# Low parts of fetched y all on GpSimd, low parts of weights meanwhile all on VectorE

## What is computed

```python
y = jnp.concatenate([ya, yb, ym], axis=-1) * jax.nn.silu(gate)   # first layer
x = x + y @ w_out_even[e]
...
y = jnp.concatenate([yc, ym], axis=-1) * jax.nn.silu(gate)       # second layer
x = x + y @ w_out_odd[o]
```

## Time and profile before

| | |
|---|---|
| median of 3 runs | 2347.54 us (2346.05 to 2352.45) |
| profiled execution | 2350.05 us, span of its instructions 2348.3 us |
| TensorE matmul busy | 2267.7 us (97%) |
| TensorE weight load busy | 1929.2 us (82%) |
| VectorE busy | 1595.3 us (68%) |
| ScalarE busy | 1311.1 us (56%) |
| GpSimd busy | 683.4 us (29%) |
| mean granted TensorE clock | 0.995 |

### The profile page before, as it was taken

How to read it: one execution, slowest core, us unless ns; L and a number is a source line. 1 busy time by engine, 2 the same in 40 slices (tenths; PEclk the granted TensorE clock), 3 DMA queues, 4 the chain that set the end, 5 groups by cost and what they waited for, 6 DMA issues and landing times.

```text
span 2348.3 us, 35371 instructions
## 1 busy us (share of the span) xinstructions
PE 2267.7 (97%) x11778; PEld 1929.2 (82%) x11778; DVE 1595.3 (68%) x3262; ACT 1311.1 (56%) x3038; POOL 683.4 (29%) x843
## 2 busy tenths in 40 slices
PE   7999999999999999999999999899999999999999
PEld 6888788888888878888888888787787888887887
DVE  7443677777886433346665566658888888889787
ACT  6444566666775434456656566654656645455542
POOL 3455232311245542222222221565563200000000
PEclk9999999999999999999999999999999999999999
DMA  7322111111243342223232322533343632345734
GB/s 228 116 74 65 40 28 33 32 34 48 61 129 107 95 138 62 93 68 91 89 95 72 93 88 87 192 90 113 102 145 108 190 102 92 115 146 168 232 114 138
DMA packets 332355, 241.68 MB, mean 103 GB/s; under 512 B 66448, under 2 KB 284816, under 8 KB 331664
## 3 DMA queue, kind: packets, MB, share of 16 engines
q1 hardware_dynamic: 332176, 239.43, 33.6%
HBM read 195.59 MB, written 43.78 MB: 102 GB/s over the span
## 4 chain that ended last, share of the span: by engine, by line
PE 78%; DVE 11%; ACT 4%; issue 3%; DMA 2%; SPq 1%; POOL 1%; DVEq 0%; ACTq 0%; POOLq 0%
PE PS L1938 14%; PE PS L1940 14%; PE PS L1939 14%; PE PS L2168 6%; PE PS L2170 6%; PE PS L2169 6%; PE PS L2084 5%; PE PS L2051 5%; PE PS L2038 3%; PE PS L2039 2%; ACT PY L2179 1%; PE PS L2093 1%; PE PS L1993 1%; PE PS L2075 1%; DVE ST L2547 1%
## 5 line engine op out<-in xcount | busy, mean ns | idle before, releaser
L2844 POOL TENSOR_TENSOR WS<-WR,WS 128x256 fp32r<-128x256 f32 x635 | 491.9, 794 | 995.8 <-ACT WS L2179 993.1
L1938 PE MATMUL PS<-HT,WS 128*128 128x512 f32 x1492 | 601.6, 403 | 15.6 <-POOL WS L2844 5.5
L1940 PE MATMUL PS<-HT,WS 128*128 128x512 f32 x1492 | 583.9, 391 | 0.0
L1939 PE MATMUL PS<-HT,WS 128*128 128x512 f32 x1492 | 581.7, 390 | 0.0
L1938 PEld LDWEIGHTS PS<-HT,WS 128*128 128x128 f32 x1492 | 280.9, 188 | 73.1 <-issue 10.4
L1940 PEld LDWEIGHTS PS<-HT,WS 128*128 128x128 f32 x1492 | 280.3, 188 | 61.4
L1939 PEld LDWEIGHTS PS<-HT,WS 128*128 128x128 f32 x1492 | 281.4, 189 | 52.0
L2179 ACT ACTIVATE PT<-PS 128x512 fp32r<-128x512 f32 x352 | 186.2, 529 | 199.2 <-PE PS L2051 198.7
L2179 ACT ACTIVATE WS<-WR 128x256 fp32r<-128x256 f32 x658 | 245.6, 410 | 91.0 <-PE PS L1940 55.2
L2437 DVE TENSOR_TENSOR PT<-PS,PT 128x512 fp32r<-128x512 f32 x352 | 211.2, 609 | 84.7 <-ACT PT L2179 81.8
L2084 PE MATMUL PS<-PT,QKV 128*128 128x256 f32 (+1 forms) x1248 | 208.8, 289 | 3.2 <-DVE YB L2616 2.3
(11 more groups left out here) (284 smaller groups left out, 4573.2 us busy)
## 6 DMA issues: line engine op xcount, KB each, us to landing
WR<-in_w_in_odd SPq DMA_DIRECT2D x106, 256.0 KB, 2.9
EO<-in_grid SPq DMA_DIRECT2D x48, 384.0 KB, 3.0
WR<-in_ffn_in SPq DMA_DIRECT2D x60, 256.0 KB, 3.0
WR<-in_w_in_even SPq DMA_DIRECT2D x100, 128.0 KB, 2.5
WR<-in_w_out_odd SPq DMA_DIRECT2D x48, 256.0 KB, 2.9
yd<-PY SPq DMA_DIRECT2D x44, 256.0 KB, 3.4
EO<-in_ffn_in SPq DMA_DIRECT2D x35, 256.0 KB, 3.0
WR<-in_w_in_even SPq DMA_DIRECT2D x34, 256.0 KB, 2.9
```

The costliest lines, as they stand in the source:

```text
L1938: e.matmul(out, wh, rh, start=start, stop=False)
L1939: e.matmul(out, wh, rl, start=False, stop=False)
L1940: return e.matmul(out, wl, rh, start=False, stop=stop)
L2844: e.tensor_tensor(ws(i, 1, n), RAW[raw_slot(u)][:, o:o + n], f32(ws(i, 0, n)), ALU.subtract).then_inc(s_wlop.sem, 1)
```

## The change

A new entry of the planner's state, `at["back"]`, is set from the start of the last chunk to the end of the products that run beside it. While it is set, every new weight split gives its low part to VectorE (`s_wlov`); before, GpSimd had them all here (the other condition, `at["second"]`, is not yet set in these two layers). And all low parts of fetched y are GpSimd's (`s_ylp`), where every second one was VectorE's. The list of steps, the high parts, the transfers, the buffers and the matmuls are the same.

```diff
             def last_chunk(att, upto, end, loads):
                 left, owed = 16, 0.0
+                at["back"] = True
                 next(loads)
...
             run_upto(end)
+            at["back"] = False
             ht_after[0] = (s_mm, s_mm.n)
...
                 if no < at["both"]:
                     on = s_wlov if no % (2 if no < 2 * MEM_UNITS else 3) else s_wlop
                 else:
-                    on = s_wlov if at["second"] and no >= at["second"] and no % 4 == 3 else s_wlop
+                    on = s_wlov if at["back"] or at["second"] and no >= at["second"] and no % 4 == 3 else s_wlop
                 half_lo.append((on, on.add()))
                 put("split", no)
...
                     s_yh.add()
-                    on = s_ylv if back % 2 else s_ylp
+                    on = s_ylp
                     i, d = landed[back]
```

More of the change, by code:

```diff
@@ L367, in build @@
         units, subs, half_lo, used = [], [], [], {}
-        at = {"load": 0, "split": 0, "both": 0, "bank": 0, "ys": 0, "slot": 0, "task": 0, "gen": None, "piece": 0, "rope": False, "f1": False, "one": False, "deep": None, "second": None}
+        at = {"load": 0, "split": 0, "both": 0, "bank": 0, "ys": 0, "slot": 0, "task": 0, "gen": None, "piece": 0, "rope": False, "f1": False, "one": False, "deep": None, "second": None, "back": False}
         raw_at = []
```

## The result

The changed kernel takes 2356.82 us (2354.06 to 2358.93) beside 2348.63 us for the kernel before (2346.05 to 2352.45). The ratio is 1.0036, with a 95% interval of 1.0025 to 1.0047, so it is slower by 8.5 us (5.9 to 11.0). That lies above my range. The profiled execution took 2358.05 us, with a span of 2356.1 us against 2348.3.

The account below looks back on a forecast made before the run. TensorE, 78% of the chain that ended last, was taken as the bound. First layer -0.5 and second layer +1.1 summed to +0.6 us, with clock 0: 2348.1 us as a median, range 2341.5 to 2353.5.

Parts of the forecast that it names:

- The bound: Two stages, one per layer: TensorE idle 5.1 and 10.2 us, clock falls 3.4 us, 18.7 us at stake in all.
- my signs: What the new profile should show, such as idle of both stages together at 15 to 17 us.
- the wait at L2093: Second layer, TensorE before transposes: 2.8 us now, weight load issued 2.1 us later, so +1.5 us; over 5 would favour (B).
- (B): Rival: y parts in a row on GpSimd delay fetches and weight loads through SyncE, 8.4 us slower, 2355.9 us; chance 0.12.
- Who changes hands: Per layer, 36 weight parts to VectorE and 11 y parts to GpSimd: VectorE busy +7.7 us, GpSimd -12.5 us.
- The holding: VectorE ops with two SBUF inputs and GpSimd ops lock a shared port; a weight part beside y costs up to 1.37 us.
- First layer: Sum of the first layer's stage: y4 to y7 about 0, the wait before 700.79 +0.2, other waits gone; -0.5 us.
- the wait at 700.79: First layer, TensorE's 1.81 us wait for a GpSimd weight part; forecast to change by +0.2 us.
- the two smaller waits there: First layer, TensorE's other two waits for GpSimd weight parts behind a y part, 0.7 us, forecast to go.
- Second layer: Sum of the second layer's stage: +0.2 + 1.5 - 0.6 = +1.1 us, bounds -3 and +4.
- Clock: TensorE's clock falls to half in both stages: change taken as 0, bounds -3.4 (both gone) and +1.7 us (one more).
- (A): Rival: TensorE's 5.5 us weight waits and 1.2 us y4 wait go, clock stays up; up to 10.1 us faster, 2337.4; chance 0.20.

Follow-up runs that it names:

- four fills: The changed kernel with each GpSimd low part of y replaced by four fills of 256 columns, which read no SBUF: 2345.47 us, ratio 0.9990 to the kernel before.

## Why the prediction was wrong

**The bound** held. The loss is idle time and clock of the same two stages; outside them the matched instructions drift by under 1.5 us. Of my signs, idle of both stages together came out at 20.2 us in the two windows of 80 us, where I had said 15 to 17, and the wait at L2093 stayed under the 5 us that would have spoken for (B).

**Who changes hands** held in count. VectorE's busy time seems to agree too: +7.7 us forecast for each layer, +7.0 in the 80 us of the first, +7.7 in the second. That is luck, since the changed kernel does less of its work within the same 80 us. Over the whole span VectorE's busy time grew by 20.8 us (1595.3 to 1616.1), 10.4 for each layer, as my sum had priced every part as if nothing held it. GpSimd's fell by 30.2 us (683.4 to 653.2), 15.1 for each layer against my 12.5: in the kernel before its own instructions were being held as well.

**The holding** I had read, with its 1.37 us and with the exclusive lock of the Trainium skill (SBUF — State Buffer, section "SBUF: two separate sides"). The same page of the Trainium skill (section "Who interferes with whom") says that a VectorE instruction with two SBUF inputs contends with a GpSimd instruction that reads SBUF and not with one that only writes it. The fills bear that out (0.43 us at most beside them). The 1.37 us I had called about the rest of the GpSimd instruction plus 0.42; by the earlier trace rows the rest was 1.16, so the sum is 1.58. But I used the holding as a price of one weight part here and there, and the adds of the sink, with two SBUF inputs too, had no price at all. I never counted what it would hold in total, and this is the step that failed: the sum of the first layer came to -0.5 us, with VectorE's late weight parts at +0.2 us, where TensorE waited 8.3 us for them. The groups of VectorE by line, 680 to 765 us (count | busy us, mean ns): first the kernel before, then the changed one, then the one with four fills.

```profile
L2675 DVE TENSOR_TENSOR HT<-PY,HT 128x512 fp32r<-128x512 f32 x5 | 6.5, 1295 | 2.8 <-ACT HT L2179 2.8
L2675 DVE TENSOR_TENSOR HT<-EO,HT 128x512 fp32r<-128x512 f32 x3 | 4.8, 1607 | 0.0
...
L2576 DVE TENSOR_TENSOR ST<-ST 128x1 f32<-128x1 f32 x18 | 2.8, 155 | 0.0
L2675 DVE TENSOR_TENSOR QKV<-EO,QKV 128x512 fp32r<-128x512 f32 x2 | 2.7, 1368 | 1.1 <-ACT QKV L2179 1.1
...
L2675 DVE TENSOR_TENSOR QKV<-PY,QKV 128x512 fp32r<-128x512 f32 x1 | 0.9, 857 | 0.3 <-ACT QKV L2179 0.3
```

```profile
L2470 DVE TENSOR_TENSOR WS<-WR,WS 128x256 fp32r<-128x256 f32 x36 | 23.7, 701 | 6.9 <-ACT WS L2181 6.9
...
L2578 DVE TENSOR_TENSOR ST<-ST 128x1 f32<-128x1 f32 x18 | 5.9, 330 | 0.0
```

```profile
L2470 DVE TENSOR_TENSOR WS<-WR,WS 128x256 fp32r<-128x256 f32 x36 | 13.6, 418 | 13.3 <-ACT WS L2181 13.3
...
L2578 DVE TENSOR_TENSOR ST<-ST 128x1 f32<-128x1 f32 x18 | 2.8, 154 | 0.0
```

In the kernel before, VectorE was held for 14.9 - 11 x 0.68 = 7.4 us in y parts, which TensorE needs later than the next weight part, and next to nothing elsewhere; the adds had none (155 ns). In the changed kernel it is held for 23.7 - 13.6 = 10.1 us in weight parts and 5.9 - 2.8 = 3.1 in adds. The total nearly doubles, and it moves to parts that TensorE needs next.

**First layer, -0.5 us forecast, 6.6 measured with this layer changed alone (5.9 in the matched traces).** I followed the early batches of y with care (y4 to y7, and the wait at 700.79) and found little there. Rightly: the wait that was 1.81 us is 1.4 us now. (For y6 and y7 I wrote 0.6 us later where my own subtraction gave 0.5; it changes nothing.) I gave the later pairs no line of their own. The two new waits, 4.95 us at 713.49 and 1.9 us near 736, both stand behind a finish of attention whose adds meet a row of y parts. Held time is about half of the first, and 1.6 us of the second (adds of 0.80 and 1.11 us in place of 0.16). I had said of the two smaller waits there "they go"; they went, and larger ones came in their place.

**Second layer, +1.1 us forecast, about 2 by difference** (8.5 - 6.6, with some 3 us of uncertainty). The matched traces show 3.4 us, of which the longer fall of the clock is 1.7. The chain that I named was right. The wait at L2093 grew from 2.8 to 3.6 us, against my +1.5, and by way of a late weight load. Two weight parts on VectorE, held to 2.20 us together, ended at 1501.43; but SyncE had a y fetch ahead of the load, issued at 1501.22 once GpSimd's y part had freed its buffer, and this ended last, as I had said. SyncE issued the load at 1501.64 and ScalarE idled 2.45 us for it (the last line is SyncE's waits, 1498 to 1502 us):

```profile
1499.23 2.20 DVE L2470 TENSOR_TENSOR WS<-WR,WS 128x256 fp32r<-128x256 f32 x2 [0.94 <-ACT WS L2181]
...
1501.22 0.32 SPq L2971 DMA_DIRECT2D PY<-yd  x1
1501.64 1.21 SPq L2917 DMA_DIRECT2D WR<-in_w_out_odd  x1
...
1506.07 0.42 ACT L2181 ACTIVATE WS<-WR 128x256 fp32r<-128x256 f32 x1 [2.45 <-DMA WR<-in_w_out_odd]
...
1507.84 0.66 PE L2095 MATMUL PS<-ID,RW 128*128 128x128 f32 x2 [3.61 <-DVE QKV L2439]
```

```profile
SPq L61 <- POOL HT L2890: 5.0, 2, 3.9
```

With four fills the wait at L2093 is still 3.2 us, so the holding is the lesser part of this chain. y parts late on GpSimd cost 3.6 us in seven waits, more than the 2 us I named, and 2.0 us with four fills. Where the holding shows in this layer is again TensorE's wait for weight parts, 3.0 us, and 1.2 with four fills.

**Clock, 0 forecast, bounds -3.4 and +1.7; +3.4 us in the profiled executions** (1.7 us in each layer). Outside my bounds: I allowed for one more fall, not for falls of twice the length. How much of it belongs to the change is less sure. With the first layer changed alone, the second shows 0.96 as well, and not the 0.98 of the kernel before, with the same order of steps:

```profile
1475.00:1565.00 90.00, 79.62 (x402) 66.00 (x401) 50.39 (x124) 47.18 (x122) 46.78 (x53) 0.96 0.46 146
```

**The rivals.** (A) had the weight waits of 5.5 us right as waits for GpSimd, and they ended, but nothing of that reached TensorE. (B) had nearly the right time, 2355.9 us, and mostly by luck, since its mechanism carried a part at most. The second layer's L2093 shows it. The first layer shows it as well: ScalarE's longest wait for a weight transfer grew from 2.7 to 4.8 us, ahead of TensorE's longest wait. But with four fills the longest is still 4.3 us and the loss is gone.

**The chances.** I gave slower by over 0.3% 0.05. The row of the 1.37 us instruction, a median of 1.25 against a minimum of 0.67, and 36 short instructions put beside a row of 22 long ones were all before me. They called for a rival in which the held time, not the busy time, decides.

## What to carry to other kernels

When work is moved between VectorE and GpSimd, price every instruction with two SBUF inputs that stays or lands beside GpSimd's reads, the one-column ones too, and ask which of them the bound engine needs next. A minimum far under the median in one line of the profile is such a price, already printed. Held time on a buffer filler costs little: 7.4 us of it in the first layer of the kernel before, and 2.3 us of loss in both layers together. Ahead of the bound engine's next operand it costs far more: 13.2 us in the first layer of the changed kernel, and 10.8 us of loss in both layers.

## What the hardware showed that I had not expected

- An instruction of one column was held about as long as one of 256: 0.16 us alone, 0.77 to 1.12 us for the four that began beside a y part on GpSimd. As an add of a per-partition scalar four that began so took 0.20 to 0.21 us.
- Fills on GpSimd held nothing: 34 weight parts that began while a fill ran took 0.40 to 0.43 us. Beside subtractions of the same length they took 0.77 to 1.52 us.
- GpSimd was slowed in turn: its y parts in the changed kernel took 1.48 us at the most against 1.26 at the least, and in the kernel before up to 1.73.
- A subtraction of 128x512 took 0.68 us on VectorE alone and 1.29 us on GpSimd. With all 22 y parts on VectorE and the weights on GpSimd the kernel was as fast as with the y parts shared (ratio 0.9999).
- The falls of the granted clock to half were 3.4 us of loss in two stages of the kernel before and 6.8 in the changed one, one execution of each (0.98 against 0.96 over 90 us, twice).
